# ScalarE and VectorE operations issued without a wait for the engine's own previous operation

## What is computed

```python
def rms_norm(x, g):
    return x * lax.rsqrt(jnp.mean(x * x, axis=-1, keepdims=True) + EPS) * g

# block 1: adaLN modulation, a projection, GLA and SSD scans in both directions, a merge
h_lat = modulate(rms_norm(x_lat, norm_mix_pre), m_lat[0], m_lat[1])
y_ctx, y_lat = hybrid_mixer(h_ctx, h_lat, rows, w_in, conv_w, ...)
x_lat = x_lat + m_lat[2] * rms_norm(y_lat, norm_mix_post)
f_lat = swiglu(modulate(rms_norm(x_lat, norm_ffn_pre), m_lat[3], m_lat[4]), w_gate, w_up, w_down)

# block 2, twice: input projection, q/k norms and rope, causal attention of 8 heads, gated output
c_q, c_kv = rmsnorm(c_q_raw, g_qa), rmsnorm(c_kv_raw, g_kva)
q, k = rmsnorm(q, g_qn), rmsnorm(k, g_kn)          # each with rope on 32 of its 96 columns
o = softmax(q k^T / sqrt(96), causal) v
```

## Time and profile before

| | |
|---|---|
| median of 3 runs | 3422.88 us (3419.71 to 3426.69) |
| span of the profiled execution | 3419.4 us |
| PE / PEld busy | 3277.4 us (96%) / 2595.7 us (76%) |
| DVE / ACT / POOL busy | 1814.9 us (53%) / 1404.1 us (41%) / 250.5 us (7%) |
| chain that ended last | PE 84%, DVE 9%, ACT 3%, DMA 2%, issue 1% |

### The profile page before, as it was taken

One profiled execution on the slowest core, in us unless ns is written; L12 is line 12 of the kernel. 1 busy time (PEld: TensorE's weight loads), 2 busy tenths in 40 slices (PEclk: granted clock), 3 DMA queues, 4 the chain that ended last, 5 costly groups with the idle time before them and its releaser, 6 DMA issues.

```text
span 3419.4 us, 45983 instructions
## 1 busy us (share of the span) xinstructions
PE 3277.4 (96%) x18179; PEld 2595.7 (76%) x18179; DVE 1814.9 (53%) x2425; ACT 1404.1 (41%) x2235; POOL 250.5 (7%) x302
## 2 busy tenths in 40 slices
PE   6899978999999999999999999999999999999999
PEld 6577645777878877889955569999999555687887
DVE  6777576556443454446664564444546645644433
ACT  4442455544332333233445553333334455433322
POOL 1000211600000000000030000000000300000001
PEclk9999989999999999999999999999999999999999
DMA  6445212133333324323200112342432001123333
GB/s 235 162 150 159 79 51 88 38 124 135 93 117 119 96 94 161 99 87 120 79 28 7 44 44 87 115 143 86 139 135 67 28 7 44 47 90 126 108 97 113
DMA packets 97767, 328.39 MB, mean 96 GB/s; under 512 B 11456, under 2 KB 12880, under 8 KB 96784
## 3 DMA queue, kind: packets, MB, share of 16 engines
q1 hardware_dynamic: 77120, 252.55, 23.2%
q0 software_dynamic: 18896, 68.63, 5.7%
q10 hardware_dynamic: 1536, 4.26, 0.3%
HBM read 299.19 MB, written 26.21 MB: 95 GB/s over the span
## 4 chain that ended last, share of the span: by engine, by line
PE 84%; DVE 9%; ACT 3%; DMA 2%; issue 1%; DVEq 0%; ACTq 0%; POOL 0%; POOLq 0%
PE psum L146 82%; DVE mixer L175 2%; DVE mixer L185 2%; PE psum L149 1%; DVE wlo L175 1%; DVE junk L189 1%; DVE arena L175 1%; ACT whi L163 1%; DMA stage<-in_wi 1%; ACT arena L154 1%; DVE region L175 0%; DMA mixer<-in_wm 0%; ACT mixer L154 0%; ACT mixer L155 0%; DMA hold<-in_wq 0%
## 5 line engine op out<-in xcount | busy, mean ns | idle before, releaser
L146 PE MATMUL psum<-region,whi 128*128 128x260 f32 (+2 forms) x7616 | 1834.4, 334 | 6.4 <-DVE region L185 3.2
L146 PEld LDWEIGHTS psum<-region,whi 128*128 128x128 f32 (+1 forms) x7616 | 1279.8, 187 | 172.6 <-DVE region L175 9.6
L146 PE MATMUL psum<-region,wlo 128*128 128x260 f32 (+2 forms) x3808 | 1266.9, 333 | 0.0
L175 DVE TENSOR_TENSOR wlo<-stage,whi 128x1024 fp32r<-128x1024 f32 (+2 forms) x454 | 512.8, 1130 | 636.5 <-ACT whi L163 602.0
L146 PEld LDWEIGHTS psum<-region,wlo 128*128 128x128 f32 (+1 forms) x3808 | 712.0, 187 | 78.2
L163 ACT CAST whi<-stage 128x1024 fp32r<-128x1024 f32 (+2 forms) x454 | 441.9, 973 | 243.3 <-PE psum L146 163.0
L154 ACT ACTIVATE arena<-psum 128x512 f32<-128x512 f32 (+2 forms) x412 | 193.2, 469 | 720.4 <-PE psum L146 715.8
L146 PE MATMUL psum<-arena 128*128 128x512 f32 (+11 forms) x1072 | 382.1, 479 | 2.7 <-ACT arena L154 2.2
L163 ACT COPY arena<-psum 128x260 f32<-128x260 f32 (+9 forms) x345 | 154.1, 447 | 376.0 <-PE psum L146 357.9
L175 DVE TENSOR_TENSOR arena<-arena 128x512 f32<-128x512 f32 (+8 forms) x341 | 212.2, 622 | 140.3 <-ACT arena L154 129.5
L175 DVE TENSOR_TENSOR arena<-arena,psum 128x512 f32<-128x512 f32 (+1 forms) x220 | 126.1, 573 | 285.0 <-PE psum L146 277.2
(11 more groups left out here) (167 smaller groups left out, 2746.0 us busy)
## 6 DMA issues: line engine op xcount, KB each, us to landing
stage<-in_w SPq DMA_DIRECT2D x144, 512.0 KB, 3.5
stage<-in_wi SPq DMA_DIRECT2D x55, 512.0 KB, 4.3
stage<-in_wo SPq DMA_DIRECT2D x48, 512.0 KB, 3.6
stage<-in_wg SPq DMA_DIRECT2D x44, 512.0 KB, 3.5
stage<-in_wu SPq DMA_DIRECT2D x44, 512.0 KB, 3.5
stage<-in_wm SPq DMA_DIRECT2D x42, 512.0 KB, 3.6
stage<-in_wd SPq DMA_DIRECT2D x32, 512.0 KB, 3.5
arena<-xr_scratch POOLq DMA_DIRECT2D x5, 2080.0 KB, 10.1
```

The lines of the kernel that those rows point to most:

```text
L146: return Issued(self, self.e and self.e.matmul(out, w, x, start=start, stop=stop, skip_group_check=True))
L175: return Issued(self, e and e.tensor_tensor(out, a, b, op))
```

## The change

The helpers get a parameter `own=True`; with `own=False` they use the engine without calling `own`, so the operation has no wait for its predecessor. Some 60 calls on ScalarE and VectorE pass it. No operation is added, removed or moved, and `last` is still noted, so the next operation that keeps its own wait waits for the newest one. Three calls that lose it get a wait for the older operation of their own engine whose result they read.

```diff
-    def copy(self, out, a):
-        e = self.own()
+    def copy(self, out, a, own=True):
+        e = self.own() if own else self.e
...
-        e.copy(W.halves(u)[0], W.staged(u)).then_inc(*W.hi.up(u))
+        e.copy(W.halves(u)[0], W.staged(u), own=False).then_inc(*W.hi.up(u))
...
-        e.tensor_tensor(lo, W.staged(u), hi.bitcast(F32), ALU.subtract).then_inc(*W.lo.up(u))
+        e.tensor_tensor(lo, W.staged(u), hi.bitcast(F32), ALU.subtract, own=False).then_inc(*W.lo.up(u))
...
-            e.tensor_tensor(hl[:, k, 0:N], tmp[:, k, 0:N], hh[:, k, 0:N].bitcast(F32), ALU.subtract).then_inc(
+            e.tensor_tensor(hl[:, k, 0:N], tmp[:, k, 0:N], hh[:, k, 0:N].bitcast(F32), ALU.subtract, own=False).then_inc(
...
+                e.wait_ge(*D["in", j])
+                e.tensor_tensor(y0, y0, psum[:, b, :], ALU.add, own=False).then_inc(*D.up("yi", j))
...
+                    if LEVEL[n - 1][1] != 64:
+                        e.wait_ge(*D["lv", n - 1])
+                    else:
+                        e.wait_ge(*D["lv", n - 2])
...
-        e.scalar_tensor_tensor(n.dst[:, k], n.x[:, k], n.A[:, k:k + 1], n.rs, ALU.mult, ALU.mult).then_inc(
+        e.scalar_tensor_tensor(n.dst[:, k], n.x[:, k], n.A[:, k:k + 1], n.rs, ALU.mult, ALU.mult, own=False).then_inc(
...
-        e.tensor_tensor(h.lo[:, k], h.src[:, k], hi, ALU.subtract).then_inc(*D.up("lo", h.key, k))
+        e.tensor_tensor(h.lo[:, k], h.src[:, k], hi, ALU.subtract, own=False).then_inc(*D.up("lo", h.key, k))
...
-            e.copy(m.q1[1], m.qT[:, h, NM:L2]).then_inc(*A.up())
+            e.copy(m.q1[1], m.qT[:, h, NM:L2], own=n < 2).then_inc(*A.up())
```

More of the change, by code:

```diff
@@ L149, in transpose, with activation @@
         return Issued(self, self.e and self.e.transpose(out, a, ident))
-    def activation(self, out, a, func, scale=1.0, bias=None):
-        e = self.own()
+    def activation(self, out, a, func, scale=1.0, bias=None, own=True):
+        e = self.own() if own else self.e
         if bias is None:
@@ L933, in act_proj @@
                     if half == 0:
-                        e.copy(vt[:, base // 128 + t, :], ps).then_inc(*A.up("tok", ch, half, t))
+                        e.copy(vt[:, base // 128 + t, :], ps, own=False).then_inc(*A.up("tok", ch, half, t))
                     else:
@@ L937, in act_proj @@
                             e.wait_ge(*evd[ring % 2][ring - 2])
-                        e.activation(ev[:, ring % 2, :], ps, ACT.Silu).then_inc(*A.up("tok", ch, half, t))
+                        e.activation(ev[:, ring % 2, :], ps, ACT.Silu, own=False).then_inc(*A.up("tok", ch, half, t))
                         A.mark("ring", ring)
@@ L1765, in act_out @@
         e.wait_ge(*sgla.pe["turn", j])
-        e.activation(hi, y, ACT.Copy, scale=P["glan"]).then_inc(*sgla.act.up("out", j))
+        e.activation(hi, y, ACT.Copy, scale=P["glan"], own=False).then_inc(*sgla.act.up("out", j))
     def dve_out(e, j):
@@ L2057, in act_norm @@
         d = n.sq4[:, 0:2] if k == 0 else n.sq4[:, 2:4]
-        e.activation(d, n.x[:, 2 * k:2 * k + 2], ACT.Square).then_inc(*A.up("sq", n.key, k))
+        e.activation(d, n.x[:, 2 * k:2 * k + 2], ACT.Square, own=False).then_inc(*A.up("sq", n.key, k))
     if what == "root":
@@ L2693, in do @@
                     e.wait_ge(*T[key, ci])
-                    e.copy(dst, psum[0:rows, bank.of[key, ci], 0:HC]).then_inc(*A.up(key, ci))
+                    e.copy(dst, psum[0:rows, bank.of[key, ci], 0:HC], own=False).then_inc(*A.up(key, ci))
             rounds(l, half, e, bs, "act", do)
@@ L3023, in act_row @@
             e.wait_ge(*rowd[c][l, n - 1])
-        e.copy(m.row[:, c, :], psum[0:4, bank.of["row", l, n, c], 0:128]).then_inc(*A.up("row", n, c))
+        e.copy(m.row[:, c, :], psum[0:4, bank.of["row", l, n, c], 0:128], own=False).then_inc(*A.up("row", n, c))
     def act_out_of(e, l, n, ch):
@@ L3378, in dve_lay2 @@
                     e.wait_ge(*A[key, ci])
-                    e.tensor_tensor(g, g, src[:, k, ts], ALU.mult).then_inc(*D.up("yg", l, half, z, k, ci))
+                    e.tensor_tensor(g, g, src[:, k, ts], ALU.mult, own=False).then_inc(*D.up("yg", l, half, z, k, ci))
                 for ci in range(m.nc):
```

172 lines of the change are left out of this document (87 added, 85 removed).

## The result

The changed kernel takes 3366.49 us (median of 4 runs, 3364.89 to 3369.67) against 3423.56 us (3419.71 to 3426.69) for the kernel before, timed beside it: ratio 0.9835 (95% interval 0.9823 to 0.9846). The profiled span falls from 3419.4 to 3365.6 us, by 54 us.

What follows compares the result with a forecast made beforehand. TensorE was taken as the bound, busy 3277 of 3419 us, with gains only in VectorE's and ScalarE's chain links: 42.7 - 4 - 7 = about 31 us, so 3392 us; range 3376 to 3413 us.

Steps and rivals of the forecast that it cites:

- TensorE's own links: Links from one TensorE operation to the next in the chain; the forecast had no gain for them.
- Mechanism and count of links: 283 changed same-engine chain links, 181 on VectorE and 102 on ScalarE, each save their gap and gain an overlap.
- The sum before deductions: Favourable-end gains over all changed chain links and those released by another engine: together 42.7 us.
- those released by others: 29 changed chain pieces released by another engine, each saving about 0.06 us of separate wait, 1.7 us.
- VectorE gets only about half of the 0.08 us: Deduction of 7 us on 181 VectorE links: an ordinary operation reads a tile from memory before it can write.
- TensorE takes over: Deduction of about 4 us where links are denser than TensorE's idle time, as at 516 to 548 and 1626 to 1633 us.
- the price of a link: At the favourable end, VectorE 0.17 us (separate wait) or 0.10 (inside); ScalarE 0.18 or 0.12.
- the cap: Activation halves, 1626 to 1633 us: seven links summing to 1.4 us limited to 1.0 us by TensorE's recorded idle.
- the rival: Slower by the clock, 400 to 590 us: earlier starts make the 1.2 GHz level hold longer; 3430 us, chance 0.05.
- The favourable end: Ordinary operations overlap like accumulator reads, 0.08 us on VectorE and 0.10 on ScalarE; all 42.7 us, put at 3378 us.
- The signs that were named: Separate waits fall, operation counts stay, row period below 0.70 us, TensorE idle 400-846 us about 46, feed-forward busy within 1 us.
- More than 10 us behind 2001 us: Sign that the forecast is wrong: stretches after 2001 us gain more than 10 us.

Runs made afterwards that it cites:

- VectorE alone: Changed kernel with ScalarE's calls keeping the own wait, so only VectorE's changed calls lose it: 3389.82 us, ratio 0.9906 to the kernel before.
- the two forecasts above: Forecast link gains for the changed kernel's rule on VectorE only (28.6 us) and on ScalarE only (16.5 us); these runs measured 3389.82 and 3403.35 us.
- The activation halves alone: Kernel before with the own wait left out only where activations are split into halves: 3412.96 us, ratio 0.9978.

## Why the prediction was wrong, step by step

Three steps failed: VectorE's overlap was halved, a link was priced too low, and TensorE's own links were put at nothing. The first two alone would have left the time inside the range; the third, most of all the clock, took it out.

- **Mechanism and count of links: right.** The sum before deductions had 41.0 us for the same-engine links (25.5 on VectorE, 15.5 on ScalarE) and 1.7 us for those released by others; measured are 27.3, 14.8 and 1.9 us. That the first number comes so close is in part luck, as the next but one point shows.
- **"VectorE gets only about half of the 0.08 us": wrong, 7 us.** The measured overlap is 83 ns at the median, in all three kinds of link, the value of the accumulator read in the earlier trace rows. The argument that an ordinary operation must first read a tile had no row behind it. VectorE alone shows it: 31.6 us. The Trainium skill (VectorE: DVE Perf Modes, The DRAIN you can't avoid) would have left VectorE nothing from its own waits; here the trace and this run disagree with it for float32 elementwise work, and its section Two Vector instructions with no wait between them, by which an unheld one starts earlier, fits instead. The Trainium skill (ScalarE: Activation LUTs, What ACT_TABLE_LOAD costs) has about 93 ns of overlap; the 95 to 102 ns here agree.
- **"TensorE takes over" (4 us) and the price of a link: two errors that cancel.** A link was priced with the 0.02 us of the earlier trace rows and costs 35 ns, and so on for each kind; at the measured medians the 283 links are worth 45.1 us (the 28.6 and 16.5 us of the two forecasts above), 4.1 us more than the 41.0. They gave 42.1, so 3.0 us were given back on them, as at 541.55 us, where the operation now waits 0.73 us for TensorE, and 2.7 us more at matmuls released by VectorE: 5.7 us, against 4. So TensorE does take over, by about the size deducted, but not at the place that the deduction was read from. There TensorE's recorded idle between activation rows was 0.2 us, so I capped seven links at 1.0 us; they gave 1.57 us. The recorded length of the group of two matmuls, 0.51 us, holds standing time too: rows that wait for nothing are 0.36 us apart, so the true slack in a period of 0.83 us was 0.47 us. The activation halves alone refute the cap.
- **TensorE's own links: put at nothing, 10.6 us without the chance part.** 7.7 us are the clock, with the wrong sign: the rival let it cost time and said against itself that the gaps get shorter; that very sentence was the reason for a gain, and I priced none. The earlier trace rows had the price: 0.87 over 190 us, and 661 against 410 ns a matmul. 3.3 us are waits hidden in TensorE's recorded work, which the count of links in the chain could not see, and 0.4 us were lost before 400 us.
- **The sum again.** Forecast 31.7 us; 7 us for the overlap, 4.1 for the price of a link, 0.2 for those released by others, 7.7 for the clock, 3.3 for hidden waits and 2.5 by chance, less 1.7 given back beyond the 4, less 0.4 and 0.5 (kept links): 53.9 of 54.0 us. The median lay 4.2 us above the traced span before and 0.9 us above it after, which is the last 3 us of the 57. The favourable end was also added up wrongly: all 42.7 us give 3380 us and not 3378, and no term of the forecast could bring the time below it.
- **The signs that were named.** Separate waits and operation counts: as said. The row period fell to 0.61 us (below 0.70). TensorE's idle from 400 to 846 us fell from 59.1 to 40.9 us, not to 46. Feed-forward busy time fell 0.9 us, within 1 us. "More than 10 us behind 2001 us" came true with 11.9 us: 5.0 us of VectorE's links there, 3.7 of ScalarE's and 3.4 of TensorE's.

## What to carry to other kernels

An own-engine wait costs little by its instruction and much by its meaning: it holds the next operation until the one ahead has ended, which cost 0.12 to 0.22 us for each link on VectorE here and 0.13 to 0.20 us on ScalarE. Count the same-engine links of the chain, price them from recorded ends and starts and with unwaited neighbours of the trace, and don't lower that price without a row. A matmul group can hold a standstill inside: take the slack from the spacing of unwaited neighbours, not from recorded idle; and where PEclk is below 1.00 just behind idle stretches, give the clock a term of either sign.

## What the runs showed of the hardware beyond what was expected

- Ordinary float32 operations overlap with the one ahead by 83 ns on VectorE and 95 to 102 ns on ScalarE, and are recorded 5 to 8 ns shorter than when they wait.
- A separate wait whose condition is already true is free behind a running operation: 2022 more of them cost nothing that can be measured.
- The order in which one operation's waits are written is worth some 11 us (ratio 0.9966, 0.9952 to 0.9980) in the kernel before, with no wait added or removed.
- The granted clock's low stretches come back at the same work in a second execution (507, 547 and 1841 us), and in the changed kernel, whose TensorE makes the same matmuls, the clock at this work is 1.00.
